# Two-block transformer on one core: 96-column sums in the norms, and constant multiplications where TensorE waits

## The chip, the cores and the metric

The kernel runs on one core of a Trainium2 chip (trn2). The metric is the device time of one execution in microseconds (us). TensorE (PE in the rows; PEld is its weight load) multiplies, VectorE (DVE), ScalarE (ACT) and GpSimd (POOL) do the element-wise work, and the SP queue issues the DMAs.

## The reference

Input `x` has 512 tokens of width 1024. Three transformer layers follow one another, and every linear starts from what a norm gives:

```python
# first block, two layers
h = fox_attention(x)  or  diff_attention(x)
x = layer_norm(DN_ALPHA * x + h)              # norms a0 and a1
f = conv_ffn(x)                               # 1024 -> 5632 -> 2816 -> 1024
x = layer_norm(DN_ALPHA * x + f)              # norms f0 and f1
...
# second block, one layer
h = rms_norm(x, norm1_pre)                    # norm c0
mixed = ...                                   # attention and a state-space branch
x = x + rms_norm(mixed, norm1_post)           # norm m
h2 = rms_norm(x, norm2_pre)                   # norm p
x = x + rms_norm(ffn, norm2_post)             # norm f, the last one
```

A layer norm needs the mean and the mean square of each token over its 1024 features, an RMS norm the mean square alone.

## The kernel before

Activations are kept feature-major: a tile of 128 features by 512 tokens is a block, and there are eight blocks `j` of an activation. Every linear is done in three products per 128 features (high part by high part, low by high, high by low), each a 128x512 product of TensorE. The weights come in units of up to 1 MB by DMA into `RAW`; ScalarE makes the high part `HI`, VectorE or GpSimd the low part `LO`. A Python planner writes one list of steps (the agenda), and each engine runs its own share of it in that order; TensorE never goes past a step whose wait is still open.

A norm is this sequence. Squares and sums of the first seven blocks are added into `A2` (squares) and `A1` (values) while the last linear still runs; the last block's value goes into `A1`, its square stays in `SQ`. Then, on TensorE, `stat0` multiplies `A2` by a column of `MEAN` (all entries 1/1024), `statm` `A1`, and `stats` `SQ`: that is a sum over the 128 partitions for each of four groups of 128 tokens. VectorE and ScalarE turn the sums into mean, variance and reciprocal deviation, and `stat1` and `stat3` spread mean and deviation over the partitions by four products of 128 columns each, `stat1` into bank 5 and `stat3` into bank 6. RMS norms have no `statm` and `stat1`. Every fp32 product stands in the trace as two matmuls, so four products are "x8" there.

After that ScalarE copies the mean out of its bank (L1852), VectorE subtracts it from the first two blocks (L2290) and GpSimd from the others (L2807), VectorE scales each block (L2298), ScalarE adds the bias and writes `XH` (L1856), VectorE writes `XL` (L2303). The next linear's first unit runs block by block behind this (`m2`: per block four products with `XH`, then two with `XL`), and the unit after it needs its `LO` parts. In norm f1 the blocks pass through ScalarE twice (L1845, L1847), since norm c0 follows at once.

The eight places: a0, f0, a1, f1 are layer norms and m an RMS norm, all between two linears, with TensorE waiting; f ends the kernel. For c0 and p the next linear starts unscaled and the sums are made beside it (`deviation`).

PSUM bank 5 holds the mean, bank 6 the deviation; linears rotate through banks 0 to 4 and 7.

Of the kernel before, what the change touches and what calls it, by code (L numbers as in the profile page):

```python
# [11 lines left out]
BF16 = mybir.dt.bfloat16  # L12
ALU = mybir.AluOpType
ACT = mybir.ActivationFunctionType
# [134 lines left out]
GROUPS = ((0, 4, 1), (2, 3))  # L149
CONV = (8, 9, 10, 11, 0, 1, 2, 3, 4, 5, 6, 7)  # L150
BEFORE = 13
QPLACE = {0: 3, 4: 4, 1: 5, 5: 6, 6: 7}


# [213 lines left out]
def agenda():  # L368
    ag = Agenda()
    steps, tiles, order = ag.steps, ag.tiles, ag.order  # L370
    places, _ = unit_places()
    sequence = unit_sequence()
    freed = [None] * 8
    lin = {"n": 0, "banks": [0, 1, 2, 3, 4, 7]}
# [8 lines left out]
    def put(*step):  # L383
        steps.append(step)
        return step

    def at_bank(step, bank):
        ag.bank_of[step] = bank
        ag.free_of[step] = freed[bank]
# [182 lines left out]
    def accumulate(n, j, mean):  # L572
        put("acc", n, j, mean)

    def statistics(n, mean):
        at_bank(put("stat0", n, mean), 6)
        if mean:
            at_bank(put("statm", n), 5)
        put("stats", n, mean)
        if mean:  # L580
            put("stat1", n)
        put("stat2", n, mean)
        put("stat3", n, mean)
        freed[6] = ("srs", ("stat2", n, mean))
        if mean:
            freed[5] = ("smub", ("stat1", n))
# [674 lines left out]
def program(nc, xT, wall, small, cfp, cmask, outT):  # L1261
    ag = agenda()
    places, _ = unit_places()
    sm, nsm = small_table()
    SEM = {n: nc.alloc_semaphore(name=f"s_{n}") for n in sorted({name for name, _ in ag.count})}
# [2 lines left out]
    s_rot = [nc.alloc_semaphore(name=f"rot{x}_in") for x in range(2)]  # L1268
    s_in, s_tab, s_sm, s_out = (nc.alloc_semaphore(name=n) for n in ("in_const", "in_tables", "in_small", "out_done"))

    s_av, s_vv, s_gv = (nc.alloc_semaphore(name=n) for n in ("own_act", "own_dve", "own_pool"))

    def when(name, *step):
# [6 lines left out]
    def sb(name, n, dt, off, parts=128):  # L1280
        return nc.alloc_sbuf_tensor_at(name, [parts, n], dt, offset=FIRST + off)
# [5 lines left out]
    TN = sb("TN", 128, F32, base)  # L1287
    LAMT = sb("LAMT", 64, F32, base + 512)
    NEGC = sb("NEGC", 32, F32, base + 768)
# [11 lines left out]
    PS = [nc.alloc_psum_tensor(f"PS{i}", [128, 512], F32) for i in range(8)]  # L1301

    IDN, UPP, LOW, MEAN, BLK, ONE = (FP[:, 128 * i:128 * i + 128] for i in range(6))
    ONE512 = FP[:, 640:1152]
    COSA, SINA, COSB, SINB = (FP[:, 1152 + 512 * i:1664 + 512 * i] for i in range(4))
    IDB, CAUS, CHNK = (MK[:, 128 * i:128 * i + 128] for i in range(3))
    MF, MB = MK[:, 384:896], MK[:, 896:1408]
# [26 lines left out]
    aMX, aNM, aSU, aRC = (sb(n, 64, F32, o + 107 * K + 256 * i) for i, n in enumerate(("aMX", "aNM", "aSU", "aRC")))  # L1334

    aNB, aNC = sb("aNB", 1024, F32, 4608), sb("aNC", 512, F32R, 4608 + 4 * K, 48)

    bVH, bVL = sb("bVH", 2048, F32R, o), sb("bVL", 2048, F32R, o + 8 * K)
    bQS = sb("bQS", 6144, F32R, o + 16 * K)
# [61 lines left out]
    NORM = {}  # L1401
# [8 lines left out]
    MU, VAR, RSD = TN[:, 92:96], TN[:, 36:40], TN[:, 40:44]  # L1410
# [73 lines left out]
    def tensor(e):  # L1484
        def mm(out, a, b, start=True, stop=True):
            return e.matmul(out, a, b, start=start, stop=stop)  # L1486

        for step in ag.steps:
            kind, a = step[0], step[1:]
            bank = ag.bank_of.get(step)  # L1490
            if step in ag.free_of and ag.free_of[step] is not None:
                e.wait_ge(*when_(ag.free_of[step]))
            if kind in ("mm", "mt"):
                T, kk = ag.tiles[a[0]], a[1]
                i, k = T.parts[kk]
                n = places[ag.order[i]][2]
# [9 lines left out]
                if kind == "mm":  # L1506
# [4 lines left out]
                    m = mm(o, lo[:, w], blk(xh, kk), False, stop)  # L1511
                else:
# [5 lines left out]
                    m = mm(o, xh[:, t], lo[:, w], False, stop)  # L1518
# [3 lines left out]
            elif kind == "m2":  # L1522
# [3 lines left out]
                n = places[ag.order[i]][2]  # L1526
# [24 lines left out]
            elif kind == "stat0":  # L1551
                n, mean = a
                nb = NORM[n]
                if mean or n in ("c0", "m", "p", "f"):
                    e.wait_ge(*when("cd", "cst"))
                mm(PS[6][:, 0:4], IDN, NEGC[:, 8:12], True, False)
                sem, count = when("ac", "acc", n, 6, mean)
                e.wait_ge(sem, count - 1 if mean else count)
                for c in range(4):
                    mm(PS[6][:, c:c + 1], nb["A2"][:, 128 * c:128 * c + 128], MEAN[:, 0:1], False, False)  # L1560
            elif kind == "statm":
                n, = a
                e.wait_ge(*when("a7", "acc", n, 7, True))
                for c in range(4):
                    m = mm(PS[5][:, c:c + 1], NORM[n]["A1"][:, 128 * c:128 * c + 128], MEAN[:, 0:1])
                m.then_inc(SEM["sma"], 1)
            elif kind == "stats":
                n, mean = a
                e.wait_ge(*when("sq", "acc", n, 7, mean))
                for c in range(4):  # L1570
                    m = mm(PS[6][:, c:c + 1], NORM[n]["SQ"][:, 128 * c:128 * c + 128], MEAN[:, 0:1], False, c == 3)
                m.then_inc(SEM["ssum"], 1)
            elif kind == "stat1":
                n, = a
# [8 lines left out]
                m.then_inc(SEM["spr"], 1)  # L1583


            elif kind == "nb":
                h, = a
                if h == 0:
# [208 lines left out]
    def scalar(e):  # L1797
        act = e.activation
        av = 0
        for step in ag.steps:  # L1800
# [32 lines left out]
            elif kind == "stat2":  # L1833
                n, mean = a
                eps = EPS5 if mean else EPS6
                if mean:
                    e.wait_ge(*when("svar", "stat1", n))
                    act(VAR, VAR, ACT.Sqrt, bias=eps).then_inc(SEM["ssd"], 1)
                else:
                    e.wait_ge(*when("ssum", "stats", n, mean))  # L1840
                    act(VAR, PS[6][:, 0:4], ACT.Sqrt, bias=eps).then_inc(SEM["ssd"], 1)
            elif kind == "ln" and a[0] == "f1":
                n, j = a
                e.wait_ge(*when("lt", *step))
# [375 lines left out]

    def vector(e):
        vv, own, ysum = 0, {}, None

        def diff(out, x, h):

# [2 lines left out]
        for step in ag.steps:  # L2228
# [38 lines left out]
                e.tensor_tensor(NORM[n]["A1"][:, :], NORM[n]["A1"][:, :], blk(YH, 7), ALU.add).then_inc(SEM["a7"], 1)  # L2267
            elif kind == "statm":
                e.wait_ge(*when("sma", *step))
                e.tensor_copy(MU, PS[5][:, 0:4]).then_inc(SEM["smu"], 1)  # L2270
                e.wait_ge(*when("smu", *step))
                e.tensor_tensor(TN[:, 32:36], MU, MU, ALU.mult).then_inc(s_vv, 1)
                vv += 1
            elif kind == "stat1":
                n, = a
                e.wait_ge(*when("ssum", "stats", n, True))
                e.wait_ge(s_vv, vv)
                e.tensor_tensor(VAR, PS[6][:, 0:4], TN[:, 32:36], ALU.subtract).then_inc(SEM["svar"], 1)
            elif kind == "stat2":
                e.wait_ge(*when("ssd", *step))  # L2280
                e.reciprocal(RSD, VAR).then_inc(SEM["srs"], 1)
# [699 lines left out]
```

## Time and profile before

| what | us |
|---|---|
| three runs | 2297.61, 2298.28, 2305.0; median 2298.28 |
| span of the profiled execution, first to last instruction | 2284.7 |
| TensorE busy | 2165.1 (95%) |
| VectorE, ScalarE, GpSimd busy | 1161.7, 1006.4, 944.3 |
| chain of work that ended last | TensorE 83%, VectorE 7%, ScalarE 4%, GpSimd 2% |
| mean granted clock of TensorE | 0.975 |

For the profiled execution the span is what is known; the median of the runs lies 13.6 us above it, which is what lies around the span. In the views a granted clock of 1.00 is 2.4 GHz and 0.50 is 1.2 GHz. A row of the windows view gives the stretch, its length, then for PE, PEld, DVE, ACT and POOL the busy us with the number of instructions in brackets, then the granted clock, the DMA share and GB/s. A row of the timeline gives the start, the length, the engine and line, the operation with its operands, and in square brackets the idle time ahead of it and what ended it; alike neighbours are merged as "x8".

### The profile page before, as it was taken

The page shows a single profiled execution, that of the slowest core. Times are in us where ns is not written, and L with a number is a line of the kernel's source. Part 1 is how long each engine was busy: PE and PEld are TensorE (multiplying, and loading weights), DVE is VectorE, ACT ScalarE, POOL GpSimd, SP SyncE. Part 2 cuts the span into 40 slices and gives each one's busy share as a digit, 9 for nine tenths or more (in the row PEclk, how much of TensorE's full clock was granted, in tenths as well). Part 3 has the DMA queues.
Part 4 walks back from the last instruction along what each step waited for, and adds up shares of the span by engine and source line. Part 5 has one row for each costly group of instructions (what it writes and reads, how often), then busy time and mean ns, then how long its engine had stood idle before and what let it go on. Part 6 is the DMA issues. An engine that isn't in the chain of part 4 may idle for free.

```text
span 2284.7 us, 27957 instructions
## 1 busy us (share of the span) xinstructions
PE 2165.1 (95%) x10720; PEld 1797.5 (79%) x10720; DVE 1161.7 (51%) x1852; ACT 1006.4 (44%) x2029; POOL 944.3 (41%) x714
## 2 busy tenths in 40 slices
PE   7999899999998898899999999889999999999997
PEld 6788778888877777778888878778678887888886
DVE  3545565554333768465554354676864326444322
ACT  5656444444224566344443245656543334332221
POOL 3655564343446664454333443222413343222233
PEclk9999999999998999999999998999999999999998
DMA  4111122322222221122232212101012231223221
GB/s 161 56 56 56 56 93 93 104 99 100 90 87 79 80 77 61 56 74 92 95 108 92 95 63 69 54 34 42 20 65 93 85 109 62 105 94 110 85 102 54
DMA packets 29844, 183.06 MB, mean 80 GB/s; under 512 B 3984, under 2 KB 4112, under 8 KB 11920
## 3 DMA queue, kind: packets, MB, share of 16 engines
q1 hardware_dynamic: 29712, 181.27, 23.0%
q8 instruction: 86, 1.41, 0.3%
q14 instruction: 46, 0.38, 0.1%
HBM read 174.97 MB, written 2.10 MB: 77 GB/s over the span
## 4 chain that ended last, share of the span: by engine, by line
PE 83%; DVE 7%; ACT 4%; issue 3%; POOL 2%; DMA 0%; SPq 0%; POOLq 0%; DVEq 0%; ACTq 0%
PE PS L1486 81%; PE PS L1611 1%; POOL LO L2777 1%; DVE bQS L2226 1%; PE PS L1724 0%; DVE aQS L2226 0%; POOL bROT L2830 0%; POOL bTQ L2835 0%; DVE YH L2328 0%; DVE XL L2303 0%; DVE T_f L2298 0%; PE PS L1659 0%; POOL cQ L2860 0%; POOL cROT L2852 0%; DVE bP L2530 0%
## 5 line engine op out<-in xcount | busy, mean ns | idle before, releaser
L2777 POOL TENSOR_TENSOR LO<-RAW,HI 128x512 fp32r<-128x512 f32 (+2 forms) x382 | 541.7, 1433 | 614.4 <-ACT HI L1810 614.4
L1486 PE MATMUL PS<-XH,HI 128*128 128x512 f32 (+1 forms) x1584 | 637.3, 402 | 25.4 <-DVE XL L2226 6.9
L1486 PE MATMUL PS<-XH,LO 128*128 128x512 f32 (+1 forms) x1584 | 626.0, 395 | 0.0
L1486 PE MATMUL PS<-XL,HI 128*128 128x512 f32 (+1 forms) x1584 | 619.4, 395 | 2.2 <-DVE XL L2303 2.2
L1810 ACT ACTIVATE HI<-RAW 128x512 fp32r<-128x512 f32 (+3 forms) x668 | 366.0, 608 | 171.3 <-PE PS L1486 168.0
L2226 DVE TENSOR_TENSOR LO<-RAW,HI 128x512 fp32r<-128x512 f32 (+2 forms) x286 | 303.1, 1064 | 246.3 <-ACT HI L1810 245.8
L1486 PEld LDWEIGHTS PS<-XH,HI 128*128 128x128 f32 (+1 forms) x1584 | 302.2, 191 | 88.9 <-issue 21.4
L1486 PEld LDWEIGHTS PS<-XH,LO 128*128 128x128 f32 (+1 forms) x1584 | 301.6, 190 | 66.0 <-issue 1.4
L1486 PEld LDWEIGHTS PS<-XL,HI 128*128 128x128 f32 (+1 forms) x1584 | 301.5, 191 | 64.6 <-DVE XL L2303 3.8
L1486 PE MATMUL PS<-HH,HI 128*128 128x512 f32 x528 | 205.4, 389 | 0.0
L1486 PE MATMUL PS<-HL,HI 128*128 128x512 f32 x528 | 205.4, 389 | 0.0
L1486 PE MATMUL PS<-HH,LO 128*128 128x512 f32 x528 | 205.4, 389 | 0.0
L1486 PE MATMUL PS<-HI,XH 128*128 128x256 f32 (+1 forms) x416 | 138.1, 332 | 13.0 <-ACT bTQ L1994 4.1
L2818 POOL TENSOR_TENSOR UT<-UT 128x512 f32<-128x512 f32 x44 | 56.5, 1284 | 201.9 <-ACT UT L1880 201.9
L1878 ACT ACTIVATE UT<-PS,SM 128x512 f32<-128x512 f32 x88 | 67.7, 772 | 127.6 <-PE PS L1486 127.6
L1486 PE MATMUL PS<-LO,XH 128*128 128x256 f32 (+1 forms) x416 | 121.4, 292 | 0.0
L1486 PE MATMUL PS<-HI,XL 128*128 128x256 f32 (+1 forms) x416 | 121.2, 291 | 0.0
L1486 PEld LDWEIGHTS PS<-HH,LO 128*128 128x128 f32 x528 | 99.1, 188 | 20.7
L1486 PEld LDWEIGHTS PS<-HH,HI 128*128 128x128 f32 x528 | 99.1, 188 | 20.5
L1486 PEld LDWEIGHTS PS<-HL,HI 128*128 128x128 f32 x528 | 99.1, 188 | 20.4
L2344 DVE SCALAR_TENSOR_TENSOR UT<-PS,SM,UT 128x511 f32<-128x511 f32 x88 | 65.4, 743 | 88.9 <-ACT UT L1878 88.9
L2824 POOL TENSOR_SCALAR aP<-aP,aRC 128x128 f32<-128x128 f32 (+1 forms) x64 | 69.5, 1087 | 92.3 <-DVE aRC L2433 92.1
(404 smaller groups left out, 3301.6 us busy)
## 6 DMA issues: line engine op xcount, KB each, us to landing
RAW<-wall SPq DMA_DIRECT2D x138, 1024.0 KB, 4.8
RAW<-wall SPq DMA_DIRECT2D x24, 896.0 KB, 4.4
bROT<-bTQ SPq DMA_DIRECT2D x64, 64.0 KB, 2.0
RAW<-wall SPq DMA_DIRECT2D x5, 512.0 KB, 3.2
XF<-xT SPq DMA_DIRECT2D x4, 512.0 KB, 5.4
outT<-XR SPq DMA_DIRECT2D x8, 256.0 KB, 2.0
FP<-cfp SPq DMA_DIRECT2D x1, 1024.0 KB, 6.7
MKF<-cmask SPq DMA_DIRECT2D x1, 704.0 KB, 11.1
```

The costliest lines, as they stand in the source:

```text
L1486: return e.matmul(out, a, b, start=start, stop=stop)
L1611: m = e.transpose(PS[bank][:, 128 * kb:128 * kb + 128], aP[:, 512 * (n % 4) + 128 * kb:512 * (n % 4) + 128 * kb + 128], IDN)
L1810: act(HI[i % 2][:, c], RAW[i % 2][:, c], ACT.Copy).then_inc(SEM["hi"], 1)
L1878: act(x, PS[ag.tiles[t].bank][:, :], ACT.Identity, bias=col(f"cb{lay}", f), scale=col(f"cw{lay}2", f)).then_inc(SEM["ui"], 1)
L2226: return e.tensor_tensor(out, x, h.bitcast(F32), ALU.subtract)
L2344: e.scalar_tensor_tensor(out=x[:, 1:512], in0=ps[:, 0:511], scalar=col(f"cw{lay}1", f), in1=x[:, 1:512], op0=ALU.mult, op1=ALU.add).then_i ...
L2777: return e.tensor_tensor(out, x, h.bitcast(F32), ALU.subtract)
L2818: e.tensor_tensor(g, g, v, ALU.mult).then_inc(SEM["um"], 1)
L2824: e.tensor_scalar(p, p, aRC[:, n:n + 1], None, ALU.mult).then_inc(SEM["dg"], 1)
```

## The change

The sums `stat0`, `statm` and `stats` take 96 columns of `MEAN` in place of one, so that each result stands 96 times, and the readers take every 128th column of the bank. A product that filled the sums' bank with zeros is dropped; the first sum starts the bank instead. A step `warm` multiplies two bf16 constants (a 128x128 identity by 512 columns of a mask) into the PSUM bank that the next linear would take: twice between `stat0` and `statm`, 4 times behind `stats` in m and f, and behind `stat3` 8 times (12 in f1, none in f). At the program's start TensorE multiplies a tile of zeros, `NIL`, 16 times into bank 7; VectorE clears that tile with its first instruction. The norms c0 and p get the wide sums and no `warm`.

```diff
+SUMS = 96
...
+    def warm(n, at, count):
+        at_bank(put("warm", n, at, count), lin["banks"][lin["n"] % len(lin["banks"])])
+
     def statistics(n, mean):
         at_bank(put("stat0", n, mean), 6)
         if mean:
+            warm(n, 0, 2)
             at_bank(put("statm", n), 5)
         put("stats", n, mean)
         if mean:
             put("stat1", n)
+        else:
+            warm(n, 1, 4)
         put("stat2", n, mean)
         put("stat3", n, mean)
+        if n != "f":
+            warm(n, 2, 12 if n == "f1" else 8)
...
+        e.wait_ge(s_nil, 1)
+        for _ in range(16):
+            mm(PS[7][:, :], NIL[:, 0:128], NIL[:, :])
...
-                mm(PS[6][:, 0:4], IDN, NEGC[:, 8:12], True, False)
                 sem, count = when("ac", "acc", n, 6, mean)
                 e.wait_ge(sem, count - 1 if mean else count)
                 for c in range(4):
-                    mm(PS[6][:, c:c + 1], nb["A2"][:, 128 * c:128 * c + 128], MEAN[:, 0:1], False, False)
+                    mm(PS[6][:, 128 * c:128 * c + SUMS], nb["A2"][:, 128 * c:128 * c + 128], MEAN[:, 0:SUMS], c == 0, False)
...
+            elif kind == "warm":
+                for _ in range(a[2]):
+                    mm(PS[bank][:, :], IDB, MF)
...
-                    act(VAR, PS[6][:, 0:4], ACT.Sqrt, bias=eps).then_inc(SEM["ssd"], 1)
+                    act(VAR, PS[6][:, 0:512:128], ACT.Sqrt, bias=eps).then_inc(SEM["ssd"], 1)
...
+        e.memset(NIL[:, :], 0.0).then_inc(s_nil, 1)
```

On TensorE, at norm a0 (`aOH` is an operand of the linear ahead, `XH` of the one behind, `MK` holds the bf16 constants, `TN` mean and deviation), the order before is:

```order
L1486 MATMUL PS<-aOH,LO_60 128x512
L1486 MATMUL PS<-NEGC,FP 128x4
L1486 MATMUL PS<-FP,A_a_156 128x1 x4
L1486 MATMUL PS<-FP,A_a_155 128x1 x4
L1486 MATMUL PS<-FP,SQ_a_154 128x1 x4
L1486 MATMUL PS<-FP,TN 128x128 x8
L1486 MATMUL PS<-XH,HI_59 128x512
```

and of the change:

```order
L1498 MATMUL PS<-aOH,LO_60 128x512
L1498 MATMUL PS<-FP,A_a_157 128x96 x4
L1498 MATMUL PS<-MK 128x512 x2
L1498 MATMUL PS<-FP,A_a_156 128x96 x4
L1498 MATMUL PS<-FP,SQ_a_155 128x96 x4
L1498 MATMUL PS<-FP,TN 128x128 x8
L1498 MATMUL PS<-MK 128x512 x8
L1498 MATMUL PS<-XH,HI_59 128x512
```

The zero fill is gone, two constant products stand behind the first sums and eight between the spreading products and the next linear.

At the last norm, f, at the end of TensorE's program, before:

```order
L1486 MATMUL PS<-HH_97,LO_60 128x512
L1486 MATMUL PS<-NEGC,FP 128x4
L1486 MATMUL PS<-FP 128x1 x8
L1486 MATMUL PS<-FP,TN 128x128 x4
L2899 UNCONDITIONAL_BRANCH
```

and of the change:

```order
L1498 MATMUL PS<-HH_98,LO_60 128x512
L1498 MATMUL PS<-FP 128x96 x8
L1498 MATMUL PS<-MK 128x512 x4
L1498 MATMUL PS<-FP,TN 128x128 x4
L2917 UNCONDITIONAL_BRANCH
```

Four constant products stand ahead of the last spreading products, and none behind them.

## Rows read from the trace of the kernel before

**Rows 1.** Windows: 60 us of a feed-forward part; columns are named above.
```profile
1980.00:2040.00 60.00, 60.00 (x266) 49.67 (x266) 25.64 (x33) 17.65 (x32) 15.30 (x10) 1.00 0.29 105
```

**Rows 2.** Windows, a0 then f1: busy per engine, then granted clock, DMA share, GB/s.
```profile
302.60:306.00 3.40, 2.81 (x26) 2.76 (x25) 1.70 (x4) 2.12 (x3) 0.07 (x1) 1.00 0.41 171
306.00:309.40 3.40, 3.40 (x18) 3.40 (x18) 0.78 (x3) 0.89 (x2) 0.39 (x1) 0.50 0.00 0
...
312.80:316.20 3.40, 3.12 (x7) 2.48 (x8) 3.40 (x5) 1.51 (x3) 3.40 (x3) 0.50 0.00 0
1350.50:1353.90 3.40, 3.36 (x29) 3.39 (x30) 0.67 (x4) 2.04 (x4) 0.00 (x0) 1.00 0.83 308
```

**Rows 3.** Timeline of norm a0: start, length, engine, line, operation [idle before].
```profile
304.34 1.02 PE L1486 MATMUL PS<-FP,A_a 128*128 128x1 f32 x8 [0.59 <-DVE A_a L2267]
...
306.24 3.54 PE L1486 MATMUL PS<-FP,TN 128*128 128x128 f32 x16
...
309.90 0.75 DVE L2298 SCALAR_TENSOR_TENSOR T_a<-T_a,TN,PS 128x512 f32<-128x512 f32 x1 [0.25 <-PE PS L1486]
...
311.55 0.47 PE L1486 MATMUL PS<-XH,HI 128*128 128x512 f32 x1 [1.77 <-ACT XH L1856]
```

**Rows 4.** Timeline of norm f1.
```profile
1352.32 2.09 PE L1486 MATMUL PS<-FP,TN 128*128 128x128 f32 x16
...
1354.85 0.75 DVE L2298 SCALAR_TENSOR_TENSOR T_f<-T_f,TN,PS 128x512 f32<-128x512 f32 x1
1355.51 0.98 DVE L2290 TENSOR_TENSOR T_f<-MS_f,YH 128x512 f32<-128x512 f32 x1
...
1357.25 0.72 PE L1486 MATMUL PS<-XH,HI 128*128 128x512 f32 x1 [2.84 <-ACT XH L1847]
```

**Rows 5.** Timeline of a0: second block, end of the linear behind.
```profile
310.57 0.76 DVE L2290 TENSOR_TENSOR T_a<-MS_a,YH 128x512 f32<-128x512 f32 x1
...
323.25 0.68 DVE L2226 TENSOR_TENSOR LO<-RAW,HI 128x512 fp32r<-128x512 f32 x1
...
324.67 0.39 PE L1486 MATMUL PS<-XH,HI 128*128 128x512 f32 x1
```

**Rows 6.** Timeline of norm a1: the same places.
```profile
981.45 3.42 PE L1486 MATMUL PS<-FP,TN 128*128 128x128 f32 x16
...
985.65 1.77 DVE L2290 TENSOR_TENSOR T_a<-MS_a,YH 128x512 f32<-128x512 f32 x1
...
998.96 0.68 DVE L2226 TENSOR_TENSOR LO<-RAW,HI 128x512 fp32r<-128x512 f32 x1
...
1000.62 0.39 PE L1486 MATMUL PS<-XH,HI 128*128 128x512 f32 x1
```

**Rows 7.** Timeline of norm f0, and TensorE behind its linear.
```profile
677.18 3.01 PE L1486 MATMUL PS<-FP,TN 128*128 128x128 f32 x16
...
680.97 1.73 DVE L2290 TENSOR_TENSOR T_f<-MS_f,YH 128x512 f32<-128x512 f32 x1
...
700.62 0.58 PE L1486 MATMUL PS<-HI,XH 128*128 128x256 f32 x1 [4.12 <-ACT bTQ L1994]
```

**Rows 8.** Timeline of norm m.
```profile
1894.32 1.16 PE L1486 MATMUL PS<-FP,TN 128*128 128x128 f32 x8 [1.15 <-DVE TN L2281]
...
1895.51 0.75 DVE L2328 SCALAR_TENSOR_TENSOR YH<-YH,SM,PS 128x512 f32<-128x512 f32 x1 [1.25 <-PE PS L1486]
```

**Rows 9.** Timeline of the last norm, f.
```profile
2271.19 0.75 DVE L2328 SCALAR_TENSOR_TENSOR YH<-YH,SM,PS 128x512 f32<-128x512 f32 x1 [2.17 <-PE PS L1486]
```

**Rows 10.** Windows: the linear beside norm p, columns as in rows 2.
```profile
1923.90:1927.30 3.40, 3.40 (x11) 2.71 (x10) 0.00 (x0) 0.00 (x0) 0.00 (x0) 0.50 0.72 284
```

**Rows 11.** Timeline of the first microseconds.
```profile
6.89 0.59 PE L1486 MATMUL PS<-XH,HI 128*16 128x512 f32 x1 [6.89 <-DVE XL L2226]
...
14.76 0.19 PEld L1486 LDWEIGHTS PS<-XH,HI 128*128 128x128 f32 x1 [0.15 <-POOL LO L2777]
...
14.97 0.39 PE L1486 MATMUL PS<-XH,HI 128*128 128x512 f32 x1
```

More of the change, by code:

```diff
@@ L1269, in program @@
     s_in, s_tab, s_sm, s_out = (nc.alloc_semaphore(name=n) for n in ("in_const", "in_tables", "in_small", "out_done"))
+    s_nil = nc.alloc_semaphore(name="nil")
     s_av, s_vv, s_gv = (nc.alloc_semaphore(name=n) for n in ("own_act", "own_dve", "own_pool"))
@@ L1336, in program @@
     aNB, aNC = sb("aNB", 1024, F32, 4608), sb("aNC", 512, F32R, 4608 + 4 * K, 48)
+    NIL = sb("NIL", 512, BF16, 4608)
     bVH, bVL = sb("bVH", 2048, F32R, o), sb("bVL", 2048, F32R, o + 8 * K)
@@ L1564, in tensor @@
                 for c in range(4):
-                    m = mm(PS[5][:, c:c + 1], NORM[n]["A1"][:, 128 * c:128 * c + 128], MEAN[:, 0:1])
+                    m = mm(PS[5][:, 128 * c:128 * c + SUMS], NORM[n]["A1"][:, 128 * c:128 * c + 128], MEAN[:, 0:SUMS], c == 0, c == 3)
                 m.then_inc(SEM["sma"], 1)
@@ L1570, in tensor @@
                 for c in range(4):
-                    m = mm(PS[6][:, c:c + 1], NORM[n]["SQ"][:, 128 * c:128 * c + 128], MEAN[:, 0:1], False, c == 3)
+                    m = mm(PS[6][:, 128 * c:128 * c + SUMS], NORM[n]["SQ"][:, 128 * c:128 * c + 128], MEAN[:, 0:SUMS], False, c == 3)
                 m.then_inc(SEM["ssum"], 1)
@@ L2269, in vector @@
                 e.wait_ge(*when("sma", *step))
-                e.tensor_copy(MU, PS[5][:, 0:4]).then_inc(SEM["smu"], 1)
+                e.tensor_copy(MU, PS[5][:, 0:512:128]).then_inc(SEM["smu"], 1)
                 e.wait_ge(*when("smu", *step))
@@ L2277, in vector @@
                 e.wait_ge(s_vv, vv)
-                e.tensor_tensor(VAR, PS[6][:, 0:4], TN[:, 32:36], ALU.subtract).then_inc(SEM["svar"], 1)
+                e.tensor_tensor(VAR, PS[6][:, 0:512:128], TN[:, 32:36], ALU.subtract).then_inc(SEM["svar"], 1)
             elif kind == "stat2":
```

## The prediction

> **What bounds the kernel now.** I read the windows first. In a feed-forward part TensorE has no idle time, 266 products in 60.00 us, so one of 512 columns takes 0.226 us [rows 1]; whatever TensorE is late by when it comes out of a norm stays in the end time, since no wait follows in which it could be made up. Around the norms it is otherwise: the granted clock falls to 0.50 (1.2 GHz). In a0 the stretch with the single-column sums has PE busy for 2.81 of 3.40 us and is still followed by 3.40 us at 0.50, in which the spreading products lie; a second stretch at 0.50 lies in the linear behind, where seven products take 3.12 busy us [rows 2]. In f1 a stretch of the same sums and the sixteen 128-column pieces of the spreading products is granted 1.00 throughout [rows 2]. So 128-column fp32 products were issued with the clock up, and single-column ones alone were what stood ahead of a fall.
>
> Then the timelines, to see who waits for whom in a norm. I count from the start of the spreading products, s. In f1, at full clock, they take 2.09 us, VectorE's first scaling (L2298) starts at s+2.53 and its second block's subtraction ends at 1356.49 = s+4.17 [rows 4]. In a0 they take 3.54 us, the scaling starts at s+3.66 and waited 0.25 us for TensorE, and the next linear's first product comes 1.77 us idle later at 311.55 [rows 3]. From there it is VectorE's chain that goes block by block; TensorE at 1.2 GHz falls behind it and must catch up.
>
> **The change part by part.**
>
> *Width of the sums.* A single-column set of eight pieces takes 1.02 us [rows 3]; a 128-column set takes 1.16 us [rows 8]. So 96 columns cost between 0 and 0.14 us per set, and per norm two sets are on the path: at most 0.3 us. I take 0, because sixteen 128-column pieces in 2.09 us are 0.13 us each, which is what eight in 1.02 us are [rows 3, 4]. The dropped zero fill stood ahead of a 0.59 us wait for VectorE [rows 3] and returns nothing.
>
> *Constants.* No row shows a bf16 product of 512 columns. The nearest is the 0.226 us of rows 1, and nearly double at 0.50 (3.12 us for seven, 0.45) [rows 2]. Two take 0.45 us and fit into the 0.59 us idle ahead of `statm`. Four take 0.90 us and fit into the 1.15 us idle of m [rows 8]. Eight take 1.8 us. The idle behind the spreading products in a0 is 1.77 us now; with them 1.45 us shorter (3.54 to 2.09) and the scaling 1.13 us sooner (3.66 to 2.53) it becomes 2.1 us, so they fit, by 0.3 us. Twelve take 2.7 us and fit into f1's 2.84 us [rows 4]. So at full clock they cost nothing, and what hides them is VectorE's and ScalarE's way to the first `XH`. The bank they write is the one next in the rotation, evacuated long before, so no wait comes with it.
>
> The Trainium skill, page "TensorE: Matmul & The Clock Gate", section "Wait — 56ns, not 53.3ns?", gives 215.7 ns warm and 426.7 ns cold for 512 bf16 columns. By it eight take 1.73 or 3.41 us; the sum would not change, and no row here shows such a product.
>
> *Norm a0.* With the spreading products at full clock the second block's subtraction ends at s+4.17 as in f1, instead of at 311.33 = s+5.09. From its end to the end of the first low part of the next unit (323.93) it is 12.60 us [rows 5]; that part then ends at 306.24+4.17+12.60 = 323.01, and the unit starts 0.05 us behind it, at 323.06 instead of 324.67. TensorE is there in time: 48 products of 0.226 us from about 310.4 on are done by 321.3 without waits. Gain 1.6 us, of which 0.9 is VectorE's chain and the rest TensorE's backlog.
>
> *Norm a1.* The subtraction of the second block took 1.77 us and ended at 987.42 = s+5.97. With a0's 12.60 us behind s+4.17 the low part ends at 998.22 instead of 999.64, and the unit starts at 998.27 instead of 1000.62 [rows 6]: gain 2.35 us. If GpSimd and VectorE collide again there, 1.6.
>
> *Norm f0.* The same subtraction ended at 682.70 = s+5.52. But behind its linear TensorE sat idle 4.12 us for ScalarE's bTQ [rows 7], so its backlog is worth nothing and only the chain's advance counts: 5.52-4.17 = 1.35, less the 0.38 us by which a1's rest (12.22) is shorter than a0's: 0.95 us.
>
> *Norms f1 and m.* Their spreading products were at full clock already (2.09 and 1.16 us) [rows 4, 8]. Only the linear behind was slow, and VectorE's chain covers that. 0.
>
> *Norm f.* Nothing follows but VectorE, GpSimd and the output. VectorE starts after 2.17 us idle, where m's start came after 1.25 us [rows 8, 9]: 0.9 us, straight off the end.
>
> *Norm p.* The sums are made beside a linear, and a stretch of 3.40 us with PE busy all of it was granted 0.50 [rows 10]. With columns in the sums ahead of it I expect 1.00: 1.7 us. In c0 the clock did not fall; 0.
>
> *Start.* TensorE sat idle 6.89 us [rows 11]. Sixteen products at 0.45 take 7.2 us at most, less once the clock rises, so the first linear (24 products, from 6.89 to 14.97, 0.34 us each) starts at most 1 us later and then needs 24 x 0.226 = 5.4 us. Yet the second linear's weight load already waited 0.15 us for GpSimd's first low part, to 14.76, and its product started at 14.97 [rows 11]: no more than 0.2 us can come back, the rest turns into a wait.
>
> Sum: 1.6+2.35+0.95+0.9+1.7+0.2 = 7.7 us off the span of 2284.7, so 2277.0, and with the 13.6 us by which the runs' median exceeds it 2290.6. The program does not fix where the clock falls (in f1 it held through the same sums at which it fell in a0), so another execution before may have lost less in p or a1. I take 0.6 us off for that: **2291.2 us**.
>
> **Rivals.** *All half-clock time comes back.* The rows show about 40 us at 0.50 in and behind the norms (two stretches as in rows 2 in a0, the like in a1 and m, three in f0, one each in f1 and p, the last in f), and if TensorE bounded all of it, half would return: 2298.3-20 = 2278. Against it: VectorE's chain and the 4.12 us wait of rows 7. It would need TensorE to leave each linear last by far. The Trainium skill, same page, section "HAM oscillation — how this bites in real kernels", reckons the penalty in that way, as throttled time x (1 - 1.2/2.4). The trace disagrees in f1 and f0. Chance 0.09, in steps down to 2285.
>
> *The sums do not hold the clock.* Then the spreading products stay slow, and only p or f may gain: 2295 to 2298. For it: 0.59 us waits remain, and no row has 96 columns. Against it: rows 2, f1. Chance 0.14.
>
> *Slower: the constants run at 1.2 GHz.* If the clock is at 0.50 when the spreading products end, eight constants take 3.6 us, the first linear of a0 starts at 309.8+3.6 = 313.4 instead of 311.55, and with eight products at 0.45 and forty at 0.226 ends at 326.0 instead of 324.67: 1.3 us later. Four such norms (f0's wait hides its own), 0.7 us in f (four constants, 1.8 us into 1.15), make 5.9: 2304.2. It decides as soon as the clock falls ahead of the spreading products. Chance 0.05.
>
> *The start costs.* TensorE, done by about 12.3, now idles over 2 us ahead of 14.76; if the clock falls on that, up to 1.7 us are lost in the second linear: 2292.9. Chance 0.12; it lies inside the forecast's own range.
>
> **How the numbers follow.** The forecast has 0.60 with its own range of 2288 to 2294.5, the start rival sits beside it, the others as given. A measurement here tells 0.3% (6.9 us, that is 2291.4) from no change, and the forecast lies on that line. Faster: half of 0.72, 0.09, and a little of the rest: 0.46. Slower by 0.3% needs the third rival and more: 0.05. Within: 0.49. The range for 8 in 10 is 2286 to 2297: below, part of the first rival and 4 us of stretches outside the norms that fall differently; above, the second.
>
> **What would show it.** After the change: granted clock 1.00 from the end of the linear to the products with `XH` in a0, a1, f0, m; the sixteen pieces of the spreading products in about 2.1 us in all four; VectorE's first scaling at s+2.5; 1.25 us idle ahead of L2328 in f; no 0.50 behind p; a wait of some 2 us for L2777 near 14.8 us; f1 as before. The prediction is wrong if a set of 96-column pieces takes over 1.2 us, if the clock still falls in the norms, or if the low parts come later than TensorE's gain.

## The result, and the profile after

The changed kernel took 2291.14 us as the median of 11 runs (2284.4 to 2294.85), the kernel before 2298.28 us beside it (11 runs, 2294.46 to 2305.0). The ratio is 0.9968, 95% interval 0.9956 to 0.998: 7.1 us or 0.3% less, on the line that the prediction had drawn between a gain and no change. The forecast was 2291.2. How well that number fits is partly luck, as the sum below shows.

From the page of the profile after, busy time by engine and the chain of work that ended last:

```profile
PE 2180.4 (95%) x10766; PEld 1798.0 (79%) x10780; DVE 1160.4 (51%) x1853; ACT 1005.9 (44%) x2029; POOL 946.8 (41%) x714
...
PE 83%; DVE 7%; ACT 4%; issue 3%; POOL 2%; DMA 1%; SPq 0%; POOLq 0%; DVEq 0%; ACTq 0%
```

The shares are those of before; TensorE is busy for 15.3 us more, part of it constants. At this size of change the page tells nothing, and one has to go to the places. The timeline of norm a0 after the change, TensorE's rows (start, length, engine, line, operation, idle ahead of it).

```profile
305.34 1.03 PE L1498 MATMUL PS<-FP,A_a 128*128 128x96 f32 x8
306.41 0.38 PE L1498 MATMUL PS<-MK 128*128 128x512 bf16 x1
307.09 1.10 PE L1498 MATMUL PS<-FP,A_a 128*128 128x96 f32 x8 [0.30 <-DVE A_a L2285]
308.03 1.06 PE L1498 MATMUL PS<-FP,SQ_a 128*128 128x96 f32 x8
308.93 2.12 PE L1498 MATMUL PS<-FP,TN 128*128 128x128 f32 x16
310.88 1.89 PE L1498 MATMUL PS<-MK 128*128 128x512 bf16 x8
313.05 0.47 PE L1498 MATMUL PS<-XH,HI 128*128 128x512 f32 x1 [0.28 <-ACT XH L1873]
```

Against [rows 3]: the sets of sums stay at 1.03 to 1.10 us with 96 columns, and from the start of `statm` to s (again the start of the spreading products) it is 1.84 us, where it was 1.90. So the width is free here, as the prediction had it. The spreading products take 2.12 us where they took 3.54, the eight constants fill all but 0.28 us of a wait that was 1.77, and the first linear product comes at s+4.12 where it came at s+5.31. The other three layer norms show 2.12 us too. VectorE's rows in the same norm, and what ends it:

```profile
311.40 0.75 DVE L2316 SCALAR_TENSOR_TENSOR T_a<-T_a,TN,PS 128x512 f32<-128x512 f32 x1
...
323.44 1.62 DVE L2321 SCALAR_TENSOR_TENSOR XL<-T_a,SM,XH 128x512 fp32r<-128x512 f32 x2
...
324.98 0.68 DVE L2244 TENSOR_TENSOR LO<-RAW,HI 128x512 fp32r<-128x512 f32 x1
...
325.86 0.62 PE L1498 MATMUL PS<-XL,HI 128*128 128x512 f32 x2
...
326.31 0.39 PE L1498 MATMUL PS<-XH,HI 128*128 128x512 f32 x1
```

The low part ends at 325.66, s+16.73, where the prediction had s+16.77. But the unit starts at 326.31, s+17.38, and not 0.05 us behind the low part: TensorE is still at the products of the last block, whose low half `XL` was ready at 323.44+1.62 = 325.06. In the kernel before it was the same distance:

```profile
321.71 1.62 DVE L2303 SCALAR_TENSOR_TENSOR XL<-T_a,SM,XH 128x512 fp32r<-128x512 f32 x2
```

323.33 there, and the unit at 324.67 [rows 5], 1.34 us behind; 1.25 us behind it now.

The windows view from norm to norm (from s to s: a0 to f0, f0 to a1, a1 to f1, f1 to m, m to f; columns as in [rows 2]):

```profile
308.93:678.87 369.94, 367.78 (x1636) 302.64 (x1635) 178.83 (x215) 144.19 (x245) 156.60 (x111) 1.00 0.28 95
678.87:985.23 306.36, 271.14 (x1508) 229.15 (x1507) 186.81 (x323) 154.68 (x351) 176.14 (x145) 0.94 0.23 72
985.23:1354.33 369.10, 367.72 (x1635) 302.64 (x1635) 179.81 (x217) 144.17 (x245) 154.46 (x109) 1.00 0.27 91
1354.33:1901.50 547.17, 518.17 (x2762) 424.24 (x2770) 303.16 (x467) 272.23 (x581) 176.03 (x126) 0.97 0.18 63
1901.50:2275.10 373.60, 369.85 (x1644) 303.33 (x1645) 151.92 (x180) 118.11 (x215) 114.99 (x78) 1.00 0.24 85
```

The kernel before had 370.94, 304.27, 370.87 and 542.00 us for the first four (the starts in [rows 3, 4, 6 to 8]). The stretches that hold the norms' effect, the first and the third, are shorter by 1.00 and 1.77 us, at a granted clock of 1.00. The fourth, which holds the whole mixer of the second block, is 5.1 us longer (547.1 from s to s; the row's end is rounded up). And the profiled span as a whole has grown, from 2284.7 to 2289.8 us: the norms are shorter, but the start, the mixer between f0 and a1 (2.1 us) and that of the second block took more than they gave. Why the runs are faster all the same comes below.

At the very end and at the start (TensorE and VectorE, then TensorE and ScalarE, and ScalarE's row of the kernel before):

```profile
2275.09 1.16 PE L1498 MATMUL PS<-FP,TN 128*128 128x128 f32 x8 [0.37 <-DVE TN L2299]
2276.28 0.75 DVE L2346 SCALAR_TENSOR_TENSOR YH<-YH,SM,PS 128x512 f32<-128x512 f32 x1 [1.25 <-PE PS L1498]
```

```profile
1.17 5.92 PE L1498 MATMUL PS<-NIL 128*128 128x512 bf16 x16 [1.17 <-DVE NIL L2240]
...
14.64 0.50 PE L1498 MATMUL PS<-XH,HI 128*128 128x512 f32 x1 [2.00 <-POOL LO L2795]
...
16.16 0.63 PE L1498 MATMUL PS<-XH,HI 128*128 128x512 f32 x1
...
22.06 0.59 ACT L1949 ACTIVATE aQS<-PS 64x512 fp32r<-64x512 f32 x1 [1.67 <-PE PS L1498]
```

```profile
20.61 0.59 ACT L1932 ACTIVATE aQS<-PS 64x512 fp32r<-64x512 f32 x1
```

VectorE starts the last norm after 1.25 us of idle time instead of 2.17 [rows 9]. At the start the first linear is done early, TensorE waits 2.00 us for GpSimd, and from 16.1 us on a product takes 0.63 us: the clock has fallen. ScalarE waits 1.67 us for that linear and reads its bank at 22.06, where the kernel before did at 20.61.

The profiled execution took 2291.64 us with a span of 2289.8: 1.8 us lie around a span, not the 13.6 that the prediction added. So the profiled execution before, with its span of 2284.7, took about 2286.5 us by my estimate, and of all 98 timed runs of that kernel in this study one was as short (2286.37). The sum was made against an execution that had lost unusually little.

### The profile page after: what moved, and what is told of

Its sections match the earlier page's. It is cut to its first block, busy times and chain, and to the rows that moved or that the text cites. A ratio compares the mean times of both kernels' runs of the same rounds, so it can differ in the third digit from the quotient of the medians.

```text
span 2289.8 us, 28064 instructions
## 1 busy us (share of the span) xinstructions
PE 2180.4 (95%) x10766; PEld 1798.0 (79%) x10780; DVE 1160.4 (51%) x1853; ACT 1005.9 (44%) x2029; POOL 946.8 (41%) x714
## 4 chain that ended last, share of the span: by engine, by line
PE 83%; DVE 7%; ACT 4%; issue 3%; POOL 2%; DMA 1%; SPq 0%; POOLq 0%; DVEq 0%; ACTq 0%
PE PS L1498 81%; PE PS L1628 1%; POOL LO L2795 1%; DVE bQS L2244 1%; DVE XL L2321 1%; PE PS L1741 0%; DMA RAW<-wall 0%; DVE aQS L2244 0%; POOL bROT L2848 0%; POOL bTQ L2853 0%; DVE T_f L2316 0%; DVE YH L2346 0%; PE PS L1676 0%; ACT HI L1827 0%; DVE bP L2548 0%
```

## The experiments

They ran in three sets, each beside the kernel before, the first set on another chip than the other two. Its median was 2298.03 us in the first set (2289.25 to 2308.21, 31 runs), 2297.34 in the second (2286.37 to 2305.34, 27) and 2297.19 in the third (2290.26 to 2304.91, 17). Single runs of one kernel scatter by 3 to 4 us, so a median of a dozen is good to about 1 us, one of six to about 2 (my estimate).

| kernel | median us (runs) | ratio, 95% interval |
|---|---|---|
| changed, the result above | 2291.14 (11) | 0.9968, 0.9956 to 0.998 |
| changed, second set | 2289.52 (9) | 0.9955, 0.9939 to 0.9972 |
| changed, third set | 2292.70 (12) | 0.9978, 0.9967 to 0.9989 |
| before, unchanged, first set | 2296.17 (12) | 0.9993, 0.9979 to 1.0006 |
| wide sums alone, first | 2290.77 (8) | 0.9963, 0.9944 to 0.9982 |
| constants in the norms alone, first | 2292.61 (12) | 0.9971, 0.9959 to 0.9983 |
| constants at the start alone, second | 2300.90 (12) | 1.0014, 1.0 to 1.0027 |
| changed, no start, first | 2288.75 (12) | 0.9957, 0.994 to 0.9975 |
| changed, no start, third | 2284.69 (6) | 0.9943, 0.9925 to 0.9961 |
| changed, 16 constants, second | 2292.61 (12) | 0.9975, 0.9961 to 0.999 |
| changed, gap filled, second | 2289.22 (7) | 0.9959, 0.9944 to 0.9974 |
| no start, more sums wide, third | 2284.48 (6) | 0.9938, 0.9925 to 0.9951 |
| no start, 32 columns, third | 2286.54 (6) | 0.9955, 0.9938 to 0.9972 |

The lengths from norm to norm in the profiled executions, s to s, tell more than the totals:

| kernel | start to a0 | a0 to f0 | f0 to a1 | a1 to f1 | f1 to m | m to f |
|---|---|---|---|---|---|---|
| before | 306.2 | 370.9 | 304.3 | 370.9 | 542.0 | 374.8 |
| before, again | 309.3 | 374.3 | 303.4 | 372.6 | 543.8 | 374.8 |
| start alone | 309.3 | 374.3 | 303.5 | 372.7 | 546.9 | 375.1 |
| constants in norms alone | 309.7 | 372.3 | 304.3 | 370.8 | 547.8 | 373.2 |
| wide sums alone | 309.3 | 370.4 | 309.4 | 369.1 | 547.1 | 373.3 |
| changed | 308.9 | 369.9 | 306.4 | 369.1 | 547.1 | 373.6 |
| changed, second | 310.8 | 369.9 | 302.3 | 369.1 | 551.4 | 373.6 |
| changed, third | 311.8 | 369.9 | 302.4 | 369.1 | 550.2 | 373.6 |
| changed, 16 constants | 309.0 | 369.9 | 305.6 | 369.1 | 548.5 | 373.6 |
| changed, gap filled | 304.8 | 369.9 | 308.5 | 369.1 | 546.9 | 373.6 |
| no start | 307.9 | 369.9 | 302.4 | 369.1 | 550.1 | 373.3 |
| no start, again | 309.5 | 369.9 | 302.3 | 369.1 | 550.2 | 373.3 |
| no start, 32 columns | 310.2 | 370.1 | 303.3 | 370.8 | 541.7 | 373.3 |
| no start, more sums wide | 309.2 | 369.9 | 301.1 | 369.1 | 546.2 | 373.3 |

**The kernel before once more.** Nothing edited.

> The kernel before, unchanged, to see how far its executions differ. Its profile had a span of 2284.7 us, and the runs' median 2298.28; the profile after shows 1.8 us around a span, not 13.6, so the profiled execution before must have been some 8 us faster than any timed one. If the difference between executions is where the clock falls, this profile has a span of 2290 to 2300, with stretches at 0.50 that the first profile had not, and the ratio to before is 1.000. Rival: something else than the clock differs (DMA, ScalarE), with the same stretches at 0.50 and later steps between them.

2296.17 us, ratio 0.9993. The profiled span was 2293.8, at a mean granted clock of 0.972 where the first had 2284.7 and 0.975. Norm a0 in this execution:

```profile
306.87 1.02 PE L1486 MATMUL PS<-FP,A_a 128*128 128x1 f32 x8 [0.59 <-DVE A_a L2267]
307.76 1.65 PE L1486 MATMUL PS<-FP,SQ_a 128*128 128x1 f32 x8
309.27 3.76 PE L1486 MATMUL PS<-FP,TN 128*128 128x128 f32 x16
...
314.80 0.77 PE L1486 MATMUL PS<-XH,HI 128*128 128x512 f32 x1 [1.77 <-ACT XH L1856]
```

Here the clock falls within the last set of sums (1.65 us where [rows 3] have 1.02 for a set) and is still down at the first linear product (0.77 us). So the same program loses a different amount in a norm from one execution to the next: the second unit of a0 came at s+18.43 in the first profile and at s+20.17 in this one, that of a1 at s+19.17 and s+20.75. Up to f1 the second profile is 7.2 us longer, and it has 13.9 us more at a granted clock of 0.50 (78.8 against 64.9). The Trainium skill, page "TensorE: Matmul & The Clock Gate", section "What's actually happening", says of a kernel's start that the number of slow products varies from run to run; the two profiles show the like far behind the start.

**One half of the change at a time.** The wide sums alone (no `warm` step, no `NIL`), and the constants in the norms alone (sums one column wide, the zero fill kept, no `NIL`):

```diff
 # wide sums alone
     def warm(n, at, count):
-        at_bank(put("warm", n, at, count), lin["banks"][lin["n"] % len(lin["banks"])])
+        pass
 ...
-        for _ in range(16):
-            mm(PS[7][:, :], NIL[:, 0:128], NIL[:, :])
 # constants alone
-                    mm(PS[6][:, 128 * c:128 * c + SUMS], nb["A2"][:, 128 * c:128 * c + 128], MEAN[:, 0:SUMS], c == 0, False)
+                    mm(PS[6][:, c:c + 1], nb["A2"][:, 128 * c:128 * c + 128], MEAN[:, 0:1], False, False)
```

> The wide sums alone, no constants, no start. By my theory the sums' columns hold the clock up to the spreading products, and those carry the gain through VectorE's chain: 0.9 in a0, 1.4 in a1, 0.95 in f0, 0.9 in f, 1.7 in p, so about 6 us and 2292.5; the first linears behind the norms may still be granted 0.50. Rival: the constants hold the clock, and the wide sums alone give under 2 us (2296 or more), with spreading products of over 3 us in a0 or a1.

> Sums of one column and the zero fill as before, with the constants of the norms (2, 4, 8 or 12), no start. By my theory the clock still falls behind the narrow sums in some norms, and then eight constants at 1.2 GHz take 3.4 us and push the first linear back: 2294 to 2299. Rival: the constants are what counts: 2291.

2290.77 and 2292.61 us, so 7.3 and 5.4 us less than the kernel before. Both together and without the start (below, 2288.75 in the same set) gave 9.3. The three intervals overlap, so by the times neither half is told from the whole, nor whether the gains add up; the time of the constants alone also lies between what its theory and its rival had named. The places tell more. First the wide sums alone, in f0 and then in a0:

```profile
677.37 1.10 PE L1498 MATMUL PS<-FP,A_f 128*128 128x96 f32 x8 [1.55 <-DVE A_f L2281]
678.31 1.57 PE L1498 MATMUL PS<-FP,SQ_f 128*128 128x96 f32 x8
679.68 3.13 PE L1498 MATMUL PS<-FP,TN 128*128 128x128 f32 x16
```

```profile
309.28 2.12 PE L1498 MATMUL PS<-FP,TN 128*128 128x128 f32 x16
313.41 0.73 PE L1498 MATMUL PS<-XH,HI 128*128 128x512 f32 x1 [2.01 <-ACT XH L1870]
```

Then the constants alone, in a0:

```profile
309.72 3.01 PE L1494 MATMUL PS<-FP,TN 128*128 128x128 f32 x16
312.52 2.62 PE L1494 MATMUL PS<-MK 128*128 128x512 bf16 x8
```

With wide sums alone the spreading products are at full clock in a0, a1 and f1 and slow in f0, where TensorE sat idle for 1.55 us ahead of its `statm`; with the constants as well it sat idle there for 1.11 us, and the clock held. With narrow sums and constants they are slow in all four layer norms (3.01, 3.76, 3.66 and 2.66 us in a0, f0, a1 and f1), and over all four profiles with narrow sums in 15 of 16 (f1 in [rows 4] is the one that held). So it is mainly the sums' width that holds the clock into the spreading products. The wide sums alone also lack the product of zeros that filled the bank, which no run tries by itself; but the kernel with 32 columns below lacks it too, and its clock fell in two norms. The eight constants behind them keep it up in the linear, but that is not what decides: with the wide sums alone the clock fell at 313.4, and the second unit of a0 still came at s+17.35, as in the full change (s+17.36). VectorE's chain covers it. What the constants alone give shows behind the spreading products: against the second profile of before the second unit of a0 comes at s+18.44 instead of s+20.17 and that of a1 at s+19.14 instead of s+20.75, since the clock comes back sooner. In the stretch from s to that unit in a0, the constants alone and then the kernel before had a granted clock of 0.91 and 0.69:

```profile
309.72:328.16 18.44, 17.36 (x74) 12.52 (x74) 15.97 (x22) 8.73 (x14) 10.71 (x7) 0.91 0.00 0
```

```profile
309.27:329.44 20.17, 17.93 (x66) 14.48 (x66) 16.95 (x22) 8.77 (x14) 11.68 (x8) 0.69 0.00 0
```

From m to f they took 373.2 us where the kernel before takes 374.8. Against the first profile of before, which had lost little, a0 and a1 show no gain (s+18.43 and s+19.17).

**The start.** Alone (the narrow kernel with the 16 products on `NIL`), and taken out of the changed kernel, twice:

```diff
-        e.wait_ge(s_nil, 1)
-        for _ in range(16):
-            mm(PS[7][:, :], NIL[:, 0:128], NIL[:, :])
```

> The kernel before with the sixteen constants ahead of the first linear alone (narrow sums, nothing in the norms). Theory: the wait of 2.0 us ahead of the second linear is followed by about 3.4 us at half clock near 16 us, which puts ScalarE's first evacuation at 22 us and not 20.6, and nothing behind it takes the 1.5 us back: 2299 to 2300 us where the kernel before has 2298. Rival (the constants gain what they save, 2.4 us of half clock in the first linear): 2297 or less, the evacuation at 20.4 or earlier.

> The change without its sixteen products at the start. In the profile after, the clock fell at 16.1 us, behind a wait of 2.0 us for GpSimd's first low part, and ScalarE's first evacuation came 1.46 us later than before. If that is what the start does in every execution, this kernel is 1 to 1.5 us faster than the change (2289.7 to 2290.1). Rival: the fall at 16.1 us was this execution's, and the start returns its 0.2 us: 2291.3.

> The changed kernel without the 16 constants ahead of the first linear, once more and beside the changed kernel. Theory (the start costs what delays ScalarE's first evacuation by 1.3 to 1.5 us): 2288 to 2290 us, 1 to 2 less than the changed kernel beside it. Rival (the start costs nothing, the two differed by scatter): no difference.

> The changed kernel a third time, nothing edited, as the yardstick of this set: 2289.5 to 2292 us, and the norms as in the first two profiles (sixteen spreading products in 2.12 us).

Alone it took 2300.9 us, 3.6 more than the kernel before beside it, at the edge of what the interval tells (1.0 to 1.0027). Its profile is 3.6 us longer than the second one of before too, but not at the start: the lengths agree to 0.1 us up to f1, and the difference lies between f1 and m (546.9 and 543.8) and behind (375.1 and 374.8), where nothing was edited. So one profile places them there, and whether they belong to the start isn't shown. Taken out, the changed kernel took 2288.75 and 2284.69 us; in the third set the intervals of with (0.9967 to 0.9989) and without (0.9925 to 0.9961) don't meet. These medians lie 8.0 us apart, more than any expectation had, and only the six runs without it stand behind the lower one; the profiles of the two lie 2.7 us apart and are what can be placed. ScalarE's first read, with and without, in that set:

```profile
22.58 0.59 ACT L1949 ACTIVATE aQS<-PS 64x512 fp32r<-64x512 f32 x1 [1.61 <-PE PS L1498]
```

```profile
20.56 0.59 ACT L1946 ACTIVATE aQS<-PS 64x512 fp32r<-64x512 f32 x1
```

These two profiles have the same lengths from norm to norm to 0.1 us up to m, and 0.3 in the last, so all else being alike the start cost 2.02 us here, and 2.26 by norm a0 (311.78 against 309.52). But the fall is not certain: in the kernel with the start alone TensorE waited about as long, 2.10 us, and the clock held.

```profile
14.81 0.50 PE L1489 MATMUL PS<-XH,HI 128*128 128x512 f32 x1 [2.10 <-POOL LO L2784]
...
16.30 0.39 PE L1489 MATMUL PS<-XH,HI 128*128 128x512 f32 x1
...
20.62 0.59 ACT L1938 ACTIVATE aQS<-PS 64x512 fp32r<-64x512 f32 x1
```

With the 16 products at the start and nothing in the gap it fell in four of five profiles, without them in none of eight. The expectation of start alone named that fall, and its own profile doesn't show it: the time came out near its 2299 to 2300 us, but not by the mechanism that it named.

**The gap filled.** Nine more constants between the first and the second linear.

```diff
         put("zero")
+        put("fill")
         qkunit(0)
 ...
+            elif kind == "fill":
+                for _ in range(9):
+                    mm(PS[7][:, :], NIL[:, 0:128], NIL[:, :])
```

> The changed kernel with nine more constants, 1.95 us, between the first linear and the second, where TensorE waits 2.0 us. Theory: the clock falls near 16 us because of that wait, so it no longer falls there, ScalarE's first evacuation goes from 22.1 us back to 20.4 to 20.6, and the time to 2289 to 2290 us, as without constants at the start. Rival (the fall comes from something else, the queue's first weights or the earlier start of work): the evacuation stays near 22 us, 2291 us.

> The changed kernel once more, nothing edited, as the yardstick for the three beside it. From its first runs: 2291 us, 2289.5 to 2292.5 as a median of a dozen; the five norms take 2.12 us for the sixteen spreading products, the clock falls near 16 us, in the second linear, and ScalarE's first evacuation there stands near 22.1 us.

```profile
13.16 2.12 PE L1499 MATMUL PS<-NIL 128*128 128x512 bf16 x9
14.93 0.58 PE L1499 MATMUL PS<-XH,HI 128*128 128x512 f32 x1
...
20.80 0.59 ACT L1953 ACTIVATE aQS<-PS 64x512 fp32r<-64x512 f32 x1 [0.49 <-PE PS L1499]
```

The clock held and ScalarE read at 20.80, against 21.91 in the changed kernel beside it. So filling the wait takes the fall away, in this profile, and leaves 0.2 us because the nine constants run past the moment at which the low part is ready. In time there is nothing to tell: 2289.22 against 2289.52 beside it, where the expectation had 2289 to 2290 with the fall gone and 2291 with it.

**Sixteen constants for eight** (and 20 for twelve in f1), behind the spreading products.

```diff
-            warm(n, 2, 12 if n == "f1" else 8)
+            warm(n, 2, 20 if n == "f1" else 16)
```

> The changed kernel with 16 constants (20 in norm f1) behind the sums of squares where it has 8 (12): 1.73 us more work for TensorE in each of five norms, ahead of the first products of the next linear. Theory: the wait for VectorE's first normalised block is about 1.5 us long with eight constants, VectorE needs 16.1 us from the spreading products to the last split block, and the second unit waits for that, so the extra constants lie in cover: 2291 to 2292.5 us, second unit still 17.4 us behind the spreading products in the first norm. Rival (TensorE's own chain bounds the norm, so that each constant too many is paid for): second unit 1.5 us later in each of five norms, 2298 to 2299 us.

```profile
310.97 3.62 PE L1498 MATMUL PS<-MK 128*128 128x512 bf16 x16
314.24 0.58 PE L1498 MATMUL PS<-XH,HI 128*128 128x512 f32 x1
```

Eight more constants cost 3.62-1.89 = 1.73 us, 0.216 us each, and the first linear product comes at s+5.22 instead of s+4.12, without a wait. So the eight had left a wait of 1.73-1.10 = 0.63 us, not the 1.5 of the expectation. The second unit came at s+17.36 all the same, and at s+17.34 in a1. 2292.61 us is 3.1 more than the changed kernel beside it, with intervals that overlap, and far from the 2298 to 2299 of a norm bound by TensorE. The 1.1 us are caught up because VectorE delivers most blocks 1.70 us apart and TensorE needs 6 x 0.226 = 1.36 for one.

**How wide, and more of it.** Without the start: sums of 32 columns; and 96, with the other narrow sums wide as well (two-column sums ahead of the rotation made 40 wide, the one-column sums of the second mixer 96).

```diff
-SUMS = 96
+SUMS = 32
 # and, apart from it, more sums wide
-                        u = 8 * ROPED.index(n) + 2 * c
-                        m = mm(PS[bank][:, u:u + 2], SQ5[n][:, 128 * c:128 * c + 128], BLK[:, 0:65:64])
+                        u = 40 * (4 * at + c)
+                        m = mm(PS[bank][:, u:u + 40].rearrange("p (i n) -> p i n", n=20), SQ5[n][:, 128 * c:128 * c + 128],
+                               BLK.rearrange("p (i n) -> p i n", n=64)[:, :, 0:20])
```

> The changed kernel without the start, its sums 32 columns wide in place of 96. Theory (it takes the width near that of the spreading products, 128, for the clock to stay): the clock falls again behind the sums in two or more of the norms, whose sixteen spreading products take 3 us or more in place of 2.12, and the time goes to 2291 to 2294. Rival (anything wider than a few columns does): norms as in the changed kernel, 2288 to 2290.

> The changed kernel without the start, and with the last narrow sums made wide too: the 40 products of two columns ahead of the rotation in the third mixer are 40 columns wide (each written to its own 40 columns of the bank, every twentieth read), and the one-column sums over the squares in the second mixer 96. Theory (a wide moving operand keeps the clock at the same pitch): the stretches at half clock that begin between 1391 and 1400 us, 10 to 17 us there and up to 30.7, no longer begin there, and their time, 10 us at half clock with products at 0.21 in place of 0.11 us, comes back in part: 2284 to 2287 us. Rival (40 columns are too few, or the work there waits for VectorE and ScalarE all the same): the stretch stays, 2288 to 2290.

Spreading products with 32 columns, in a0 and in a1 of one execution:

```profile
310.18 2.12 PE L1498 MATMUL PS<-FP,TN 128*128 128x128 f32 x16
...
983.56 3.66 PE L1498 MATMUL PS<-FP,TN 128*128 128x128 f32 x16
```

They were at full clock in a0 and f1 and slow in f0 (3.46) and a1, where 96 columns held in all four in each of the eight profiles that had the constants too. The 32-column kernel took 2286.54 us, so the time that was expected of the lost clock (2291 to 2294) didn't come: in its profile the norms lost time as expected (the second units of f0 and a1 came at s+23.42 and s+19.12 instead of s+22.46 and s+17.38), but the stretch from f1 to m was 541.7 us, 8.5 less than with 96 columns. The kernel with more wide sums took 2284.48 us, as long as the one without them beside it. Its two-column sums, now 40 wide, cost next to nothing (1.06 us for a set of eight against 1.03), but the fall near 1391 us came all the same:

```profile
1389.60 1.06 PE L1498 MATMUL PS<-FP,cO 128*128 128x40 f32 x8
1391.03 2.93 PE L1498 MATMUL PS<-FP,cO 128*128 128x40 f32 x16 [0.37 <-ACT TN L2079]
```

The theory failed there, and the rival (the stretch stays) was right on the mechanism; the time lies in the theory's range all the same, but so does that of the kernel beside it without the wider sums. I haven't tried 96 columns in that place, so the width and the wait of 0.37 us ahead of it are not told apart.

In the second mixer, where the sums went from 1 column to 96, the profile does differ. Its products behind such a set, without the wider sums and then with them:

```profile
928.60 3.40 PE L1498 MATMUL PS<-FP,bST 128*128 128x128 f32 x16 [1.79 <-DVE bST L2560]
```

```profile
928.32 2.02 PE L1498 MATMUL PS<-FP,bST 128*128 128x128 f32 x16 [1.71 <-DVE bST L2561]
```

Each of the other thirteen profiles has a stretch at half clock that begins between 925 and 943 us, this one has none, and from f0 to a1 it took 301.1 us, the shortest of all. It is one profile. The other thirteen, all with one column here, differ in a way that says more: the products shown were slow (3.37 to 3.75 us) in the eight with 96 columns in the norms, and took 2.02 us in the five with 1 or 32 columns there, whose clock fell later, at 937 to 943 us. So what is done in a norm goes along with where the clock falls 250 us behind it.

## Why the prediction was right, and where it was not

**Right: what the change does to the clock.** The signs that it named are there: 1.00 granted from the sums to the products with `XH` in a0, f0, a1 and m; the spreading products in 2.12 us; the first scaling at s+2.47 (2.5 was named); 1.25 us ahead of the scaling in f; no 0.50 behind p; a wait of about 2 us for GpSimd near 14.8 us. The low part of a0 ended at s+16.73 (16.77 was worked out), and the width cost nothing. The rival that the sums do not hold the clock is refuted by the wide sums alone in three norms of four, the one of constants at 1.2 GHz by the 1.89 us for eight, and all of the half-clock time coming back (2278 us) by the times.

**The terms**, each against the same profiled execution that they were made from, as the advance of the second unit behind s:

| term | predicted | measured |
|---|---|---|
| a0 | 1.6 | 18.43-17.38 = 1.05 |
| a1 | 2.35 | 19.17-17.36 = 1.81 |
| f0 | 0.95 | 23.44-22.45 = 0.99 |
| f1 and m | 0 | 0.05 and -0.19 |
| f | 0.9 | 2.17-1.25 = 0.92 |
| p | 1.7 | 1.3 (m to f: 374.76-373.64 = 1.12, with m's 0.19) |
| start | 0.2 | -1.45 (20.61 to 22.06) |

In a0 and a1 the step "TensorE is there in time: 48 products of 0.226 us from about 310.4 on are done by 321.3 without waits" was wrong. TensorE gets most blocks 1.70 us apart, at VectorE's pace, and is done 1.25 us behind VectorE's last `XL`, later than the low part from which I had counted. Both terms were 0.55 too large for it: the part that was put down to "TensorE's backlog" did not come, since TensorE stood hardly further behind that `XL` before (1.34 us). The last split `XL` itself advanced by only 323.33-306.24-(325.06-308.93) = 0.96 us in a0.

At the start the step "no more than 0.2 us can come back, the rest turns into a wait" was right about the wait and wrong about its price; the rival "The start costs" (up to 1.7 us) is what happened, with 1.45 here and 2.02 in the third set.

**Wrong: the frame of the sum.** The step "with the 13.6 us by which the runs' median exceeds it" took one execution's shortfall for an overhead; what lies around a span is 1.8 us. Against that execution the measured terms give 1.05+1.81+0.99+0.05-0.19+0.92+1.3-1.45 = 4.5 us, not the 7.7 of the sum. A usual execution of before loses more in the norms: in the second profile the second units of a0 and a1 came 2.79 and 3.39 us later than with the change, where the first had 1.05 and 1.81, and that of f1 0.97 us later, a term that I had at 0. Against that profile the stretches behind a0, a1 and m are 4.4, 3.5 and 1.1 us shorter with the change, and the two mixers, f0 to a1 and f1 to m, 3.0 and 3.3 us longer. So the norms' gain is larger than my sum, and the start and the mixers take part of it away. These errors have opposite signs, and that the total came out to 0.1 us is luck; how the 7.1 us of the runs divide among them isn't measured.

**Open.** In the profiles the stretch from f1 to m is 542.0, 543.8 and 546.9 us with the norms as before, 547.8 with the constants and 541.7 with 32 columns, and 546.2 to 551.4 in the eight of the changed kernel and its variants with 96 columns and constants. The longer ones have more half clock: 20.5 to 23.9 us of it in the three below 544, and 30.7 to 44.4 in the others. Whether the norms, by where they leave the clock, cause that, or a few profiles don't show what usual runs do, isn't settled; the eight against five profiles in the second mixer speak for the first. The timed runs have no profile, and they are 7.1 us apart, more than these profiles (2284.7 and 2293.8 us of span against 2289.8 to 2291.9) would give. If it is the first, several us of the gain in the norms are given back there.

The version to keep is the changed kernel without the products at the start, 2288.75 and 2284.69 us: 0.4 to 0.6% below the kernel before.

## What to carry to other kernels

Where tiny products stand between TensorE's large ones, make them wide if that is free: a set of eight pieces cost 1.02 us at one column and 1.02 to 1.10 at 96, and the products behind mostly stayed at full clock. That this shortens the whole kernel is less sure than that it shortens the norm: with 32 columns the clock fell in two norms, and the time was as short. Before filling a wait with constants, ask whether the engine is what the stage waits for afterwards; a wait that is only moved (here to the gap ahead of the second linear) can be followed by a fall of the clock in a worse place. Before a sum is set against a profile, compare the profiled execution's own time with the runs: one execution is a sample, and here only one of 98 timed runs was as short.

## What the hardware showed that I had not expected

Fp32 products of the norms' sums take nearly the same time at 1, 32 and 96 columns (1.02, 0.97 to 1.06 and 1.02 to 1.10 us for eight pieces), yet in the layer norms the spreading products behind 1 column were slow in 15 cases of 16, behind 32 (with constants) in two of four, behind 96 in one of four alone and in none of 32 with constants. The places at which the clock falls differ between executions of one program, whose spans were 2284.7 and 2293.8 us. A bf16 product of 512 columns came every 0.216 us at full clock; the Trainium skill, page "TensorE: Matmul & The Clock Gate", section "Wait — 56ns, not 53.3ns?", gives 215.7 ns, and the rows of eight and sixteen agree. After a wait of 2.0 to 2.3 us at the start the clock fell in four profiles of five, and in the fifth, with 2.10 us, it did not.
